# Queries, keys and one gate: the high and the low part of u in one product of 512 columns

## What is computed

```python
u = modulate(rms_norm(x, norm_mix_g), sh_a, sc_a)
proj = u @ w_in
q_m, k_m, v_m, o_m, if_m, q_a, k_a, v_a, g_m, g_a = split(proj)
h_m = sigmoid(o_m) * norm(mlstm(silu(conv(q_m, k_m)), v_m, if_m))      # 4 heads
h_a = dilated_window_attention(q_a, k_a, v_a)                          # 12 heads, 3 patterns
y = sigmoid(g_m) * (h_m @ w_branch_m) + sigmoid(g_a) * (h_a @ w_branch_a)
x = x + gt_a * (y @ w_out)
x = x + gt_f * moe(modulate(rms_norm(x, norm_ffn_g), sh_f, sc_f))      # 16 experts, top 2
out = rms_norm(x, final_norm_g)
```

## Time and profile before

| | us |
|---|---|
| median of three runs | 603.99 (603.16 to 604.38) |
| the profiled execution | 600.97 |
| its span | 599.1 |
| granted clock of TensorE, mean | 0.997 |
| TensorE busy | 577.4 (96%) |
| VectorE busy | 306.9 (51%) |
| ScalarE busy | 238.7 (40%) |
| low parts L953, 51 of them | 114.2, mean 2.25 |
| high parts L613, 50 of them | 94.9, mean 1.91 |

### The profile page before, as it was taken

How to read it: one execution, slowest core, us unless ns; L and a number is a source line. 1 busy time by engine, 2 the same in 40 slices (tenths; PEclk the granted TensorE clock), 3 DMA queues, 4 the chain that set the end, 5 groups by cost and what they waited for, 6 DMA issues and landing times.

```text
span 599.1 us, 8462 instructions
## 1 busy us (share of the span) xinstructions
PE 577.4 (96%) x3563; PEld 423.3 (71%) x3563; DVE 306.9 (51%) x461; ACT 238.7 (40%) x330; POOL 9.0 (2%) x23
## 2 busy tenths in 40 slices
PE   3999999999999999999999999999999999999995
PEld 0789988999998888999999988533534444353432
DVE  0679976766568966677546683712212130221204
ACT  5617658444454545764683334701111020111113
POOL 3001000000000000000000000000000000000000
PEclk9999999999999999999999999999999999999998
DMA  8999664785859947636558989399999999999992
GB/s 309 387 332 323 212 206 140 282 287 209 287 209 341 328 170 279 220 107 237 198 217 318 416 341 357 154 378 423 421 419 422 423 421 419 422 421 422 421 382 78
DMA packets 51577, 184.78 MB, mean 308 GB/s; under 512 B 3649, under 2 KB 3761, under 8 KB 37713
## 3 DMA queue, kind: packets, MB, share of 16 engines
q1 hardware_dynamic: 50706, 183.53, 79.7%
q10 hardware_dynamic: 704, 0.58, 0.3%
q0 software_dynamic: 128, 0.11, 0.1%
HBM read 183.16 MB, written 1.05 MB: 307 GB/s over the span
## 4 chain that ended last, share of the span: by engine, by line
PE 90%; DVE 3%; ACT 3%; DMA 1%; issue 1%; SPq 0%; ACTq 0%; DVEq 0%
PE ps L1576 30%; PE ps L1788 18%; PE ps L1598 16%; PE ps L1800 8%; PE ps L1834 3%; PE ps L1776 2%; DMA first_ada<-in_ada_w_dram 1%; PE ps L1810 1%; PE ps L1683 1%; PE ps L1698 1%; PE ps L1662 1%; PE ps L1494 1%; PE ps L1827 1%; DVE lo L953 1%; PE ps L1587 1%
## 5 line engine op out<-in xcount | busy, mean ns | idle before, releaser
L953 DVE TENSOR_TENSOR lo<-raw,hi 128x2048 fp32r<-128x2048 f32 (+1 forms) x51 | 114.2, 2248 | 41.2 <-ACT hi L613 40.8
L1576 PE MATMUL ps<-u_hi,hi 128*128 128x256 f32 x416 | 120.3, 289 | 0.7 <-DVE lo L953 0.7
L1576 PE MATMUL ps<-u_lo,hi 128*128 128x256 f32 x416 | 117.9, 283 | 0.0
L1576 PE MATMUL ps<-u_hi,lo 128*128 128x256 f32 x416 | 117.9, 283 | 0.0
L1788 PE MATMUL ps<-ring,xe_t 128*64 128x512 f32 x512 | 111.7, 593 | 0.0
L613 ACT CAST hi<-raw 128x2048 fp32r<-128x2048 f32 x50 | 94.9, 1908 | 36.0 <-PE ps L1576 25.5
L1788 PEld LDWEIGHTS ps<-ring,xe_t 128*64 128x64 f32 x512 | 36.5, 137 | 71.7 <-issue 71.4
L1576 PEld LDWEIGHTS ps<-u_hi,hi 128*128 128x128 f32 x416 | 79.8, 192 | 2.1 <-DVE lo L953 1.1
L1576 PEld LDWEIGHTS ps<-u_lo,hi 128*128 128x128 f32 x416 | 79.9, 192 | 0.2
L1576 PEld LDWEIGHTS ps<-u_hi,lo 128*128 128x128 f32 x416 | 79.9, 192 | 0.0
L1800 PE MATMUL ps<-ring,he_t 128*64 128x512 f32 x224 | 49.6, 596 | 0.0
(11 more groups left out here) (334 smaller groups left out, 837.0 us busy)
## 6 DMA issues: line engine op xcount, KB each, us to landing
raw<-in_w_in_dram SPq DMA_DIRECT2D x41, 1024.0 KB, 5.2
ring<-in_w_gate_e_dram SPq DMA_DIRECT2D x32, 1024.0 KB, 17.4
ring<-in_w_up_e_dram SPq DMA_DIRECT2D x32, 1024.0 KB, 16.0
ring<-in_w_down_e_dram SPq DMA_DIRECT2D x28, 1024.0 KB, 16.0
raw<-in_ada_w_dram SPq DMA_DIRECT2D x16, 1024.0 KB, 5.3
first_ada<-in_ada_w_dram SPq DMA_DIRECT2D x16, 512.0 KB, 11.8
raw<-in_w_branch_m_dram SPq DMA_DIRECT2D x4, 1024.0 KB, 5.5
raw<-in_w_out_dram SPq DMA_DIRECT2D x4, 1024.0 KB, 6.1
```

The costliest lines, as they stand in the source:

```text
L953: ins = V.tensor_tensor(lo[b % RING][:, tiles, :], src[:, tiles, :], hi[b % RING][:, tiles, :].bitcast(F32), ALU.subtract)
L1576: ins = mm(dst, w[:, k, cols], x[:, k0 + k, :], start=(first and c % 2 == 0 and k == 0 and n == 0), stop=(end and k == KB - 1 and n == 2), ...
```

## The change

For the eight groups of q_a, k_a and g_m (`WIDE`), `u_hi` and `u_lo` become two halves of one tensor `u_both`, and the high part of the weights is multiplied with both in one product of 2 x 256 = 512 columns. Its result fills a whole bank: the first half of the bank collects high x high and, by a second product of 256 columns, low x high; the second half collects high x low. Each of the four quarters has a bank of its own, so a wide group takes all of banks 0 to 3, in the order 2, 3, 0, 1 for queries and keys and 0, 1, 2, 3 for the gate.

To empty it, ScalarE copies the second half of each bank into the destination (two quarters after the group's second quarter is done, `pair_done`; two at the block's end, `block_done`), and VectorE adds the first half (`halved`, `summed`; a pair at a time). For g_m ScalarE then takes the sigmoid from SBUF to SBUF. The copies stand in ScalarE's turn s behind the high part of block s+2; the sums in VectorE's turn s behind the low part of block s+2 and ahead of the ada product and the chores. The next group's first quarter waits for the first pair's sum, its third quarter for the second pair's (if it is wide itself); group 12 and group 19, which aren't wide, wait for the first pair of group 11 and 18. The emptying of q_a and k_a by ScalarE from whole banks is gone.

```diff
--- before.py
+++ after.py
@@ -67,6 +67,7 @@
 NBLK = len(BLOCKS)
 BLK_IN = 2 * len(IN_GROUPS)
 AHEAD = RING - 1
+WIDE = [_g for _g, (_kind, _, _) in enumerate(GROUP_LIST) if _kind in ("qa", "ka", "gm")]
 
 
 
@@ -156,8 +157,8 @@
         raw = [at(f"raw{i}", 8 * i, [P, KB, NB]) for i in range(RAW)]
         hi = [at(f"hi{i}", 32 + 8 * i, [P, KB, NB], F32R) for i in range(RING)]
         lo = [at(f"lo{i}", 56 + 8 * i, [P, KB, NB], F32R) for i in range(RING)]
-        u_hi = at("u_hi", 80, [P, KT, T], F32R)
-        u_lo = at("u_lo", 88, [P, KT, T], F32R)
+        u_both = at("u_both", 80, [P, 2, KT, T], F32R)
+        u_hi, u_lo = u_both[:, 0], u_both[:, 1]
         hm_hi = at("hm_hi", 80, [P, KT, T], F32R)
         hm_lo = at("hm_lo", 88, [P, KT, T], F32R)
         qk_m = at("qk_m", 96, [P, 2 * KT, T])
@@ -268,6 +269,7 @@
         first_w = [sem(f"first_w{k}") for k in range(KB - 1)]
         hi_ready, lo_ready, block_done = sem("hi_ready"), sem("lo_ready"), sem("block_done")
         evac_act, evac_dve = sem("evac_act"), sem("evac_dve")
+        pair_done, halved, summed = sem("pair_done"), sem("halved"), sem("summed")
         consts_ready, acc_zero, ones_column = sem("consts_ready"), sem("acc_zero"), sem("ones_column")
         pick_zero, pick_ready = sem("pick_zero"), sem("pick_ready")
         pool_step, act_step, dve_step = sem("pool_step"), sem("act_step"), sem("dve_step")
@@ -398,6 +400,8 @@
         conv_order = [g for g, half in CONV_AT.values() if half == 1]
 
         def evac_engine(g):
+            if GROUP_LIST[g][0] in ("qa", "ka"):
+                return "sums"
             return "dve" if GROUP_LIST[g][0] in ("qk", "bm", "ba", "wo") else "act"
 
         def banks_of(g):
@@ -405,8 +409,25 @@
             n = g if g < EARLY else (g - EARLY) % 2
             return 2 * n, 2 * n + 1
 
+        def wide_banks(g):
+
+            return (2, 3, 0, 1) if GROUP_LIST[g][0] in ("qa", "ka") else (0, 1, 2, 3)
+
+        def wide_out(g, c):
+
+            kind = GROUP_LIST[g][0]
+            j = [x for x in WIDE if GROUP_LIST[x][0] == kind].index(g)
+            return {"qa": q_a, "ka": k_a, "gm": sig_gm}[kind][:, 4 * j + c, :]
+
+        def wide_free(eng, g, pair):
+
+            eng.wait_ge(summed, 2 * WIDE.index(g) + pair + 1)
+
         def evacuated(eng, g):
 
+            if g in WIDE:
+                wide_free(eng, g, 1)
+                return
             e = evac_engine(g)
             groups = [x for x in range(len(GROUP_LIST)) if evac_engine(x) == e]
             if e == "dve":
@@ -694,21 +715,33 @@
                     A_(qk_m[:, 4 * gq:4 * gq + 4, :], qk_m[:, 4 * gq:4 * gq + 4, :], ACT.Silu).then_inc(qk_ready, 1)
                 g, _, _, end = BLOCKS[s]
                 kind, _, _ = GROUP_LIST[g]
+                if end and g in WIDE:
+                    if kind == "qa":
+                        after(act, "u_lo1_3")
+                    if kind == "gm":
+                        after(act, "m_val3")
+                    for c in range(4):
+                        if c == 0:
+                            act.wait_ge(pair_done, WIDE.index(g) + 1)
+                        if c == 2:
+                            act.wait_ge(block_done, s + 1)
+                        ins = nc.scalar.copy(wide_out(g, c), ps[wide_banks(g)[c]][:, T:2 * T])
+                        if c % 2:
+                            ins.then_inc(halved, 1)
                 if end and evac_engine(g) == "act":
-                    act.wait_ge(block_done, s + 1)
+                    if g in WIDE:
+                        evacuated(act, g)
+                    else:
+                        act.wait_ge(block_done, s + 1)
                     first = min(x for x, (n, _, _) in enumerate(GROUP_LIST) if n == kind)
                     j = g - first
                     banks = banks_of(g)
                     func = ACT.Sigmoid if kind in ("o", "gm", "ga") else ACT.Copy
                     if kind == "o" and j == 0:
                         after(act, "m_val3")
-                    if kind == "gm" and j == 0:
-                        after(act, "m_val3")
-                    if kind == "qa" and j == 0:
-                        after(act, "u_lo1_3")
                     if kind == "va" and j == 0:
                         after(act, "m_val3")
-                    dst = {"va": v_a, "o": sig_o, "qa": q_a, "ka": k_a, "gm": sig_gm, "ga": sig_ga}.get(kind)
+                    dst = {"va": v_a, "o": sig_o, "gm": sig_gm, "ga": sig_ga}.get(kind)
                     for n, bank in enumerate(banks):
                         if kind == "vm":
                             view = v_m[:, n, 2 * j:2 * j + 2, 0:MD]
@@ -717,7 +750,7 @@
                             view, src = dst[:, n, j * NB:(j + 1) * NB], ps[bank][:]
                         else:
                             view = dst[:, 4 * j + 2 * n:4 * j + 2 * n + 2, :]
-                            src = ps[bank][:].rearrange("p (c t) -> p c t", c=2)
+                            src = view if g in WIDE else ps[bank][:].rearrange("p (c t) -> p c t", c=2)
                         ins = A_(view, src, func)
                     ins.then_inc(evac_act, 1)
 
@@ -1074,6 +1107,13 @@
                 g, _, _, end = BLOCKS[s]
                 kind, col, _ = GROUP_LIST[g]
                 banks = banks_of(g)
+                if end and g in WIDE:
+                    for c in range(4):
+                        if c % 2 == 0:
+                            dve.wait_ge(halved, 2 * WIDE.index(g) + c // 2 + 1)
+                        ins = V.tensor_tensor(wide_out(g, c), ps[wide_banks(g)[c]][:, 0:T], wide_out(g, c), ALU.add)
+                        if c % 2:
+                            ins.then_inc(summed, 1)
                 if end and kind in ("bm", "ba", "wo") and s < NBLK - 1:
                     dve.wait_ge(block_done, s + 1)
                 if end and kind == "bm":
@@ -1533,8 +1573,11 @@
 
             for s, (g, k0, first, end) in enumerate(BLOCKS):
                 kind, _, channel_major = GROUP_LIST[g]
-                if first and g >= EARLY:
-                    evacuated(pe, g - EARLY if g < EARLY + 2 else g - 2)
+                if first and g >= EARLY and g not in WIDE:
+                    if g - 1 in WIDE:
+                        wide_free(pe, g - 1, 0)
+                    else:
+                        evacuated(pe, g - EARLY if g < EARLY + 2 else g - 2)
                 if g == 21:
                     after(pe, f"hm_lo{k0 // KB}")
                 if g == 23:
@@ -1556,6 +1599,22 @@
                             for n, (w, x) in enumerate(((w_hi, x_hi), (w_hi, x_lo), (w_lo, x_hi))):
                                 ins = mm(dst, w[:, k, cols], x[:, k0 + k, :], start=(first and c % 2 == 0 and k == 0 and n == 0),
                                          stop=(end and k == KB - 1 and n == 2), skip_group_check=True)
+                elif g in WIDE:
+                    for c in range(4):
+                        bank = wide_banks(g)[c]
+                        if first and c % 2 == 0:
+                            if g - 1 in WIDE:
+                                wide_free(pe, g - 1, c // 2)
+                            else:
+                                evacuated(pe, g - 2 + c // 2)
+                        cols = slice(c * P, (c + 1) * P)
+                        for k in range(KB):
+                            mm(ps[bank][:].rearrange("p (a t) -> p a t", a=2), w_hi[:, k, cols], u_both[:, :, k0 + k, :],
+                               start=(first and k == 0), stop=False, skip_group_check=True)
+                            ins = mm(ps[bank][:, 0:T], w_lo[:, k, cols], u_hi[:, k0 + k, :], start=False,
+                                     stop=(end and k == KB - 1), skip_group_check=True)
+                        if end and c == 1:
+                            ins.then_inc(pair_done, 1)
                 elif channel_major:
                     for c in range(4):
                         if s == EARLY - 1 and c == 3:
```

## The result

| | before | after |
|---|---|---|
| median, us | 604.12 (603.16 to 604.38) | 618.49 (from 617.96) |
| ratio, 95% interval | | 1.0255 (1.0225 to 1.0286) |
| the profiled execution, us | 600.97 | 618.73 |
| its span | 599.1 | 616.9 |
| granted clock, mean | 0.997 | 0.978 |

The change makes the kernel 2.5% slower: 14.4 us in the medians, 15.4 by the ratio. The forecast was 614.1 us, 10.1 more than before, with a range up to 618.5. By the medians the result is at the upper edge of that range, by the ratio (603.99 x 1.0255 = 619.4) a microsecond beyond it. One execution of after lay far above the rest under a disturbed clock and stands in neither column.

A forecast was written before the change was run, and what follows sets the result against it. TensorE was taken as the bound, never starved. Waits of 11.1 less 3.3 gained give +7.8; one clock fall of 2.3 makes +10.1: 600.97 becomes 611.1, plus 3.0 to the median, 614.1 us; range 608.5 to 618.5.

The forecast's parts named there:

- rival (d): Wide blocks: the wide product is no faster than its two halves; 617.4 us with a clock fall, 615.1 without; chance 0.10.
- the 3.3 us in all: TensorE's predicted gain over 16 wide blocks, from saving about 13 ns per pair of products.
- 0.21: Predicted gain in us per wide block, from 5.76 to 5.55 us.
- The three waits: TensorE waiting for VectorE's sums before blocks 16, 24 and 36: 2.1, 3.2 and 5.8 us, 11.1 in all.
- block 20: Transition predicted to hold without a wait, its slack near nil; named likeliest to wait over half a microsecond against the forecast.
- Rival (c): Release by pairs hides the emptying at every transition, so only the products change: 600.7 us; chance 0.08.
- one fall of 2.3 us: Granted clock drops to half once, around block 36 after the 5.8 us wait, costing 2.3 us.
- the 3.0 us: Constant added to the 611.1 us sum because the median of runs lay 3.0 above the profiled execution, giving 614.1.
- a wait shorter than 2.7 us is safe: Read from the end of the span: the clock fell some 2.7 us after TensorE went quiet.
- Rival (b): Two clock falls, or waits that each come out longer: 616.4 us and up; chance 0.10.
- my row (2.1 to 3.3): Cost in us of one clock fall, taken from slow row sums at the kernel's start; 2.3 was chosen.
- turn 13: VectorE's sums there delay m_neg and so block 16's high part by 0.8 us, leading to the 2.1 us wait.

The follow-up runs named there:

- moved: All eight groups wide as in the changed kernel, with copies and sums moved to where ScalarE and VectorE stand idle; median 603.1 us, ratio 1.0006 to the kernel before.
- before_short: The kernel before with 19 narrow products (2.3 us) left out; median 603.4 us, ratio 0.9989 to the kernel before.
- moved_late: The kernel with the emptying moved, plus ten idle 512-column products (2.3 us) ahead of block 24; median 602.9 us, ratio 0.9999 to the kernel before.
- gate_moved: The changed kernel with only the emptying of group 17 (the gate) moved, into turns 34 and 35; 611.0 us, ratio 1.0159 to the kernel before.

## Why the prediction was right and wrong

**The product.** 5.55 us a wide block in the chain, as predicted, so rival (d) is out. But the 3.3 us in all did not come: 2.5 is left for it in the profile of after and 2.3 in that of moved. Inside a block a pair takes the 0.35 us of the sum, so that u streamed in two runs costs nothing there; most blocks gain less than 0.21 from start to start, and why I have not traced. Instead of the 2.5 ns per product of the Trainium skill ("TensorE: Matmul & The Clock Gate", "Back-to-back issue gap") the trace shows again some 13: a pair of 512 and 256 columns takes 347 ns (5.55 us / 16), where 768 columns at 2.4 GHz are 320.

**The three waits.** Predicted 2.1, 3.2 and 5.8, measured 2.0, 3.4 and 5.8, at the three blocks named; block 20, which I had put on the edge, waited some 0.4. The sum is cheaper than I took it (four in 1.41 us, 0.35 each, against 0.41), which changed little, because what counts is when VectorE gets to it. The experiments that take one part alone and that move one place show each wait to hang on the place where I had put it. Rival (c) is out by these waits.

**The clock is the step that failed.** I charged one fall of 2.3 us. The profile has five, 9.9 us, which is 7.6 more, and 7.6 is also what separates the measured 618.7 of the profiled execution from the 611.1 that the sum gave for it. The median misses by 4.4 only, because the 3.0 us that I had added for it did not come (618.5 against 618.7): one error covered part of the other, by luck. Three parts of the step were wrong.

First, I read from the end of the span that a wait shorter than 2.7 us is safe. The wait of 2.0 us before block 16 brought a fall too, one microsecond after it had ended; the one of 3.4 brought one before it had ended (from 187.3). And the 2.7 us were a single row, the lowest of its kind: in the 14 profiles of this case the clock falls 2.7 to 4.9 us after the last product. The latest is that of moved, last product and stretch:

```profile
596.33 0.39 PE L1914 MATMUL ps<-y_lo_e,scat 128*128 128x512 f32 x1
```

```profile
601.00:602.00 1.00, 0.00 (x0) 0.79 1.01 389
```

Rival (b) came true, and further than I had drawn it: I gave it 0.10 and one extra fall, and left most of it outside the range.

Second, I took the price near the low end of my row (2.1 to 3.3). In the profiles here a low stretch ahead of the end of the span lasted 3.4 or 6.8 us and cost 0.9 to 1.9 or 2.5 to 3.1 us, so my range fits the long kind and not the short. The rows at the start that I took it from show a slow pace, but not a low clock: the profile gives 1.00 for that stretch.

```profile
10.00:15.00 5.00, 4.59 (x21) 1.00 1.05 387
```

Third, I had no term for the falls at old waits. The wait for mod_p and the router stand in the kernel before at full clock, and I took them as settled, because one profiled execution showed them so. And I added the 3.0 us between profiled execution and median as a constant, without asking what they were. They were most likely falls of the same sort.

**What stays open.** Why one execution of a kernel has a low clock behind mod_p and another not. before_short and moved_late speak for it that moving the later stages by 2.3 us changes the odds, whatever the product. But some profiles, of moved and moved_late among them, have a fall at 45 us, ahead of everything that was changed; that part of the difference between moved and before is not explained by the shift. Without fillers at that place, six of the nine profiles of kernels with wide groups have it, and none of the three with narrow products only. The wait for u_lo ends at 44.1 to 44.6 us in the nine and at 45.1 to 45.4 in the three, so place in time may be behind it here too, but no run tests that.

## What to carry to other kernels

An engine that is half idle is no cover for a step that somebody waits for: walk the in-order queue from the last event that it depends on to the new step, and compare with the work that the waiting engine still has. That walk was good to 0.2 us for the three long waits here (for turn 13 alone it missed 0.5), and the same walk shows where the step can go instead: into the microseconds in which that engine waits for another. And of a TensorE-bound kernel with a few short waits, one profile is one draw: look at the mean clock of every execution before you read a difference of 2 or 3 us, or add one.

## What the hardware showed that I had not expected

- The clock can fall after a wait of 2.0 us, and after it has ended, in the midst of full work (129.3 us in after), as well as behind 0.9 us of wait with one-column products after it; after a wait of 1.8 us (gate_moved) it did not. The two levels were 1.00 and 0.50 in every profile, and low stretches lasted 3.4 or 6.8 us.
- Leaving out 2.3 us of products (before_short) did not move the median (ratio 0.9989, 0.9963 to 1.0015): the best execution came 2.0 us earlier than the best of the kernel before, and nine of its eleven executions had mean clocks of 0.985 to 0.990.
- A sum of 128x256 with one operand in PSUM took 0.35 us on VectorE (four in 1.41).
